# First halves of W1 and W3 in two buffers instead of three, in the expert stage of a hybrid decoder step

## The chip, the cores and the metric

One core of one Trainium2 chip. A time is the device time of one execution in microseconds (us); the kernel before has a median of 1078.21 us over three runs (1077.11 to 1081.03). All tensors are float32.

## The reference

One layer for 512 prompt tokens and 8 decode tokens (520 rows of 1024). Three branches (gated short convolution, stick-breaking attention, cross-attention on a memory) are merged through sigmoid gates and added to the input. Then comes a mixture of 32 experts, of which each token uses two:

```
x1 = x + sum(gates * branch) @ w_o
h  = rms_norm(x1, norm2)
g_idx = argmax(h @ w_group + b_group)              # 1 of 4 groups
top_v, top_i = top_k(router logits of that group, 2)   # 2 of its 8 experts
gate = softmax(top_v) * g_prob[g_idx]
y[t] = sum over the 2 experts e of  gate * ((silu(h[t] @ w1[e]) * (h[t] @ w3[e])) @ w2[e])
out = x1 + y
```

w1 and w3 are 1024x512 for each expert and w2 is 512x1024, so each of the three is 2 MiB, 6 MiB for one expert and 192 MiB for all.

## The kernel before

The first part (to about 590 us) makes the projections, the attention branches, the merge, x1, h and the routing. The rest is the expert stage, which the change touches. In it every expert n from 0 to 31 is computed for up to 64 token slots; what does not fit goes to extra blocks at the end, run only if there are any.

TensorE runs one round for each expert, in the order written out at L1452 to L1488. In a round it first waits for the gathered and transposed rows, then does `up_and_gate` (L1381): two parts of four K chunks, each chunk two matmuls of 128x512, one for W1 (L1389) and one for W3 (L1390), which run in two halves of the array beside each other. Before each part it waits for the weights of that part, and after each part it raises the semaphore `up_ps`. Then it gives back two pieces of the expert before (`give`, L1424), transposes the activations (L776), gives back a third piece, does `down` (the W2 matmuls, L1414 and L1415), which raises `y2_ps`, and gives back the fourth. VectorE, ScalarE and GpSimd evict, activate, add the pieces to x1 and build the selection matrices beside it. GpSimd gathers the rows of two experts at a time (`xg`, an indirect DMA from `h_dram`).

The weights have three buffers each (`WS = 3`, L61; L235 to L237): expert n uses buffer n % 3 of W1, W3 and W2, called w_a, w_b, w_c in the profile (the profile's name does not tell W1 from W3 and W2; the lines do). SyncE (SP) issues all weight DMAs on one queue, in program order. `load_up` (L540) issues W1 and W3 in two parts of 1 MiB each, in the order first half of W1, first half of W3, second half of W1, second half of W3; `load_expert` (L579) then issues W2 as one DMA of 2 MiB at L583. Before each it waits for the buffer to come free: for the first halves of expert n+3 until the first part of expert n is done (`up_ps` at 2n+1), for the second halves until the second part is done (2n+2), for W2 until `down` of expert n is done (`y2_ps` at n+1). Experts 0, 1 and 2 are loaded ahead of this loop, at L552 to L577, between the DMAs of the stages before: the first and second halves of W1 of expert 2 at L568, those of W3 of expert 2 and then W2 of expert 2 at L576 and L577, when the routing has passed `row_ps`. The DMAs at L548 are all those of W1 and W3.

Of the kernel before, what the change touches and what calls it, by code (L numbers as in the profile page):

```python
# [29 lines left out]
KD = D // P  # L30
# [9 lines left out]
NE = NG * EPG  # L40
# [20 lines left out]
WS = 3  # L61
# [25 lines left out]
def build(nc, io):  # L87
    ctx = ExitStack()
    with ctx:
# [7 lines left out]
        def place(name, region, offset, shape, dt=F32):  # L97
            return nc.alloc_sbuf_tensor_at(name, [P] + list(shape), dt, offset=at[region] + offset)
# [12 lines left out]
        def sem(name):  # L111
            return ctx.enter_context(nc.semaphore(name))
# [122 lines left out]
        w1_sb = [place("w1_a", "t", 0, [KD, DE]), place("w1_b", "ws", 16384, [KD, DE]), place("w1_c", "xn", 0, [KD, DE])]  # L235
        w3_sb = [place("w3_a", "t", 16384, [KD, DE]), place("w3_b", "qk", 0, [KD, DE]), place("w3_c", "ys", 0, [KD, DE])]
        w2_sb = [place("w2_a", "ws", 0, [CW, D]), place("w2_b", "qk", 16384, [CW, D]), place("w2_c", "xn", 16640, [CW, D])]  # L237
# [39 lines left out]
        first = route("first", [1])  # L277
# [55 lines left out]
        def bank(b, n=1):  # L333
            return acc_all[:, b * 512:(b + n) * 512]
# [10 lines left out]
        def tok(tt):  # L345
# [45 lines left out]
        lg_ps, lg_ok, lg_max, lg_exp, pick_ok, rank_ps, dest_ok, ids_ps, ids_ok, over_ok = (  # L391
            sem(n) for n in ("lg_ps", "lg_ok", "lg_max", "lg_exp", "pick_ok", "rank_ps",
                             "dest_ok", "ids_ps", "ids_ok", "over_ok"))
        w13_ld = [[sem(f"w13_ld{j}{part}") for part in "ab"] for j in range(WS)]
        w2_ld = [sem(f"w2_ld{j}") for j in range(WS)]
        xgt_ps, xgt_sb, up_ps, up_ok, upt_ps, sig_ok, half_ok, actt_ok, y2_ps = (sem(n) for n in (
            "xgt_ps", "xgt_sb", "up_ps", "up_ok", "upt_ps", "sig_ok", "half_ok", "actt_ok", "y2_ps"))
# [46 lines left out]
        def _(sp):  # L444
# [72 lines left out]
            w1_d = io["w1"].rearrange("e (p k) n -> e p k n", p=P)  # L517
            w3_d = io["w3"].rearrange("e (p k) n -> e p k n", p=P)
            w2_d = io["w2"].rearrange("e (p c) n -> e p c n", p=P)
# [14 lines left out]
            for j in range(RING):  # L534
                n = 2 * KD + j
# [1 line left out]
                sp.dma_start(w_raw[:, j, :, :], io["w_in"][IN_CHUNKS + RING + n]).then_inc(w_ld[j], 16)  # L537
                load_branch(n + RING)

            def load_up(e, j, *which, before=None):  # L540


                for part in range(2):
                    if before is not None:
                        sp.wait_ge(up_ps, 2 * before + part - 1)
                    ks = slice(part * KD // 2, (part + 1) * KD // 2)
                    for tiles, dram in (which,) if which else ((w1_sb, w1_d), (w3_sb, w3_d)):
                        sp.dma_start(tiles[j][:, ks, :], dram[e][:, ks, :]).then_inc(w13_ld[j][part], 16)  # L548


            sp.wait_ge(mid_st, MID_STORES)
# [13 lines left out]
                             x1[0:NB, NT - 1, half * DE:(half + 1) * DE]).then_inc(acc_ld, 16)  # L565
            sp.wait_ge(wo_ps, NT - 1)
            load_up(1, 1, w3_sb, w3_d)
            load_up(2, 2, w1_sb, w1_d)  # L568
            sp.wait_ge(wo_ps, 2 * NT)
            load_up(0, 0, w1_sb, w1_d)  # L570
            sp.wait_ge(h_ok, NT)
# [1 line left out]
            sp.dma_start(w2_sb[1][:, :, :], w2_d[1]).then_inc(w2_ld[1], 16)  # L573
            sp.wait_ge(h_st, 16 * NT)
            sp.wait_ge(row_ps, 1)
            load_up(2, 2, w3_sb, w3_d)  # L576
            sp.dma_start(w2_sb[2][:, :, :], w2_d[2]).then_inc(w2_ld[2], 16)  # L577

            def load_expert(e, j, before):  # L579
                load_up(e, j, before=before)  # L580

                sp.wait_ge(y2_ps, before)
                sp.dma_start(w2_sb[j][:, :, :], w2_d[e]).then_inc(w2_ld[j], 16)  # L583

            with sp.Fori(0, NE // WS - 1) as i:
                for j in range(WS):
                    load_expert(WS * i + WS + j, j, WS * i + j + 1)
            for e in range(NE // WS * WS, NE):
                load_expert(e, e % WS, e - WS + 1)

            sp.wait_ge(over_ok, 1)
            n_extra = sp.value_load(over_i[0:1, EXTRA:EXTRA + 1], min_val=0, max_val=EXTRA)
            with sp.If(n_extra > 0):
                with sp.Fori(0, EXTRA // 2) as i:
                    with sp.If(n_extra > 2 * i):
                        for j in range(2):
                            e = sp.value_load(over_i[0:1, bass.ds(2 * i + j, 1)], min_val=0, max_val=NE - 1)
# [176 lines left out]
        def _(pe):  # L774
# [3 lines left out]
            def warm_up(times, b=0):  # L778

                for _ in range(times):  # L780
                    pe.matmul(bank(b)[:, 0:P], ident[:, :], ident[:, :], start=True, stop=True)
# [346 lines left out]
            for h in range(HEADS):  # L1128
                pair, second = divmod(h, 2)
                n = KD + h  # L1130
# [44 lines left out]
            with pe.Fori(0, KD // RING) as i:  # L1175
                for j in range(RING):
                    n = 2 * KD + RING * i + j
# [200 lines left out]
                    pe.wait_ge(xgt_sb, 2 * p + half)  # L1378
                turn_pair(p % 2, half)

            def up_and_gate(w, slot, j, loads, n=None):  # L1381

                for part in range(2):
                    if n == 0:
                        pe.wait_ge(row_sb, part + 2)
                    pe.wait_ge(w13_ld[w][part], 32 * loads)
                    for k in range(part * KD // 2, (part + 1) * KD // 2):
                        lhs = xg_t[:, slot, k, CAP * j:CAP * (j + 1)]
                        pe.matmul(bank(5)[0:CAP, :], lhs, w1_sb[w][:, k, :], start=(k == 0), stop=(k == KD - 1))  # L1389
                        mm = pe.matmul(bank(5)[CAP:P, :], lhs, w3_sb[w][:, k, :], start=(k == 0), stop=(k == KD - 1))  # L1390
                    mm.then_inc(up_ps, 1)
                    if n == 0 and part == 0:
                        pe.wait_ge(dest_ok, GATED)
                        find(at_pos, lambda m, r, c: pick_of[0:m, r, c, :], NE, bank(2)).then_inc(ids_ps, 1)
                    if n == 1 and part == 0:
                        pe.wait_ge(dest_ok, OVER_SET)
                        find(over_pos, lambda m, r, c: over_in[0:m, r, c, :, :].rearrange("p a b -> p (a b)"), 2 * EXTRA,
                             bank(0)).then_inc(ids_ps, 1)
# [53 lines left out]
            for n in range(NE):  # L1452
                p, j = divmod(n, 2)
                if n >= 1:
                    pe.wait_ge(xgt_sb, 2 * p + 2)
                    pe.wait_ge(up_ok, n)
                up_and_gate(n % WS, p % 2, j, n // WS + 1, n)
                if n >= 1:
                    give(n - 1, (0, 1))
                else:  # L1460
                    warm_up(2)
                pe.wait_ge(up_ok, n + 1)
                turn_up()
                if n == 0:
                    warm_up(3)
                if n == 1:
                    turn_rows(1, 0)
                elif 2 <= n < NE - 2:
                    if n > BATCH and n % BATCH == 1:
                        pe.wait_ge(few_ok, 4 * (n // BATCH))  # L1470
                    turn_rows(p + 1, j)
                if n >= 1:
                    give(n - 1, (2,))
                if n == NE - 1:
                    give(n - 1, (3,))
                if n >= 1:
                    pe.wait_ge(rest_ok, n)
                down(n % WS, n // WS + 1, n)
                if n == 1:
                    turn_rows(1, 1)  # L1480
                if 1 <= n < NE - 1:
                    give(n - 1, (3,))
                if n >= BATCH and n % BATCH == 0:
                    give_few(n // BATCH - 1)
# [8 lines left out]
            with pe.If(n_extra > 0):  # L1493
                with pe.Fori(0, EXTRA // 2) as i:
                    with pe.If(n_extra > 2 * i):
                        for half in range(2):
                            if half == 0:
                                pe.wait_ge(xg_ld[0], 16 * (PAIRS // 2 + 1) + 16 * i)
                            pe.wait_ge(xgt_sb, NE + half + 2 * i)
                            pe.sem_inc(carried_pe, 1)  # L1500
                            turn_pair(0, half)
                        pe.wait_ge(xgt_sb, NE + 2 + 2 * i)
                        for j in range(2):
                            pe.wait_ge(up_ok, NE + j + 2 * i)
                            pe.sem_inc(carried_pe, 1)
                            loads = -(-NE // WS) + 1 + j + 2 * i
                            up_and_gate(0, 0, j, loads)
                            pe.wait_ge(up_ok, NE + j + 1 + 2 * i)
                            pe.sem_inc(carried_pe, 1)
                            turn_up()  # L1510
                            pe.wait_ge(actt_ok, 2 * (NE + j) + 2 + 4 * i)
                            pe.wait_ge(rest_ok, NE + j + 2 * i)
                            pe.sem_inc(carried_pe, 1)
                            down(0, loads)
                            pe.wait_ge(spread_ok, NE + j + 1 + 2 * i)
                            pe.wait_ge(rest_ok, NE + j + 1 + 2 * i)
                            for t in range(PIECES):
                                pe.wait_ge(back_ok, PIECES * (NE + j) + t - 1 + 2 * PIECES * i)
                                pe.sem_inc(carried_pe, 1)
                                give_back(t, j, (PIECES * j + t) % 2)  # L1520
# [1182 lines left out]
```

## Time and profile before

| | us |
|---|---|
| median of three runs | 1078.21 |
| profiled execution, device time | 1076.84 |
| its span, first to last instruction | 1075.0 |
| TensorE busy | 1041.4 (97%) |
| VectorE busy | 587.0 |
| ScalarE busy | 318.9 |
| DMA moved | 278.38 MB, mean 259 GB/s |

The profiled execution lies 1.37 us below the median of the three runs. The span is cut by the page into 40 slices of 26.9 us; the expert stage fills slices 23 to 40. Landing times are counted from the start of the DMA's issue.

### The profile page before, as it was taken

What the parts mean: (1) busy time and instruction counts of PE and PEld (TensorE: products, weight loads), DVE (VectorE), ACT (ScalarE), POOL (GpSimd) and SP (SyncE); (2) the same over time, 40 slices, a digit from 0 to 9 for tenths busy, and PEclk for the clock granted to TensorE, in tenths of its full rate; (3) what the DMA queues carried; (4) which work ended last, traced back from release to release, by engine and by line L of the source; (5) the groups of instructions that cost most, each with busy time, mean ns of one, the idle gap of its engine ahead of it and who ended that gap; (6) DMA issues with size and microseconds to landing.
All of it is one profiled execution on the core that took longest, in us unless ns stands there. A gap on an engine that the chain in (4) does not pass through costs nothing.

```text
span 1075.0 us, 16267 instructions
## 1 busy us (share of the span) xinstructions
PE 1041.4 (97%) x6646; PEld 697.9 (65%) x6646; DVE 587.0 (55%) x939; ACT 318.9 (30%) x470; POOL 148.6 (14%) x180
## 2 busy tenths in 40 slices
PE   8999999999999999999999999999999999999994
PEld 8999998988868777999775444444333344433331
DVE  5222255887756765433546655556555655555555
ACT  6322242164546544322343011111111111111110
POOL 0000000012303564000000311101111110111110
PEclk9999999999999999999999999999999999999998
DMA  5622131645442232651445999999999999999962
GB/s 201 262 90 98 64 99 57 217 129 190 157 183 87 92 106 80 221 205 66 162 179 225 424 423 425 426 426 427 426 425 425 428 429 423 426 426 427 426 296 80
DMA packets 51254, 278.38 MB, mean 259 GB/s; under 512 B 7538, under 2 KB 7810, under 8 KB 30708
## 3 DMA queue, kind: packets, MB, share of 16 engines
q1 hardware_dynamic: 42516, 254.79, 58.8%
q0 software_dynamic: 6048, 16.86, 4.4%
q10 hardware_dynamic: 2624, 5.80, 1.5%
q8 instruction: 48, 0.79, 0.3%
q14 instruction: 18, 0.15, 0.0%
HBM read 274.04 MB, written 7.48 MB: 262 GB/s over the span
## 4 chain that ended last, share of the span: by engine, by line
PE 88%; DVE 4%; DMA 3%; POOL 2%; issue 2%; ACT 2%; ACTq 0%; SPq 0%; DVEq 0%; POOLq 0%
PE acc_all L809 26%; PE acc_all L1389 20%; PE acc_all L1414 10%; PE acc_all L1424 7%; PE acc_all L776 6%; PE acc_all L955 5%; PE acc_all L1202 4%; DMA vals<-in_cache_mem_v 1%; PE acc_all L1005 1%; DMA xg<-h_dram,pair_row 1%; POOL beta L437 1%; PE acc_all L1073 1%; PE acc_all L1327 1%; PE acc_all L1415 1%; PE acc_all L885 1%
## 5 line engine op out<-in xcount | busy, mean ns | idle before, releaser
L809 PE MATMUL acc_all<-xn_hi,w_hi 128*128 128x260 f32 x832 | 171.5, 287 | 6.0 <-DVE gate_sb L2114 2.4
L809 PE MATMUL acc_all<-xn_hi,w_lo 128*128 128x260 f32 x832 | 168.0, 284 | 0.0
L809 PE MATMUL acc_all<-xn_lo,w_hi 128*128 128x260 f32 x832 | 167.8, 283 | 0.0
L2554 DVE TENSOR_TENSOR x<-x,acc_all 128x1024 f32<-128x1024 f32 x128 | 152.7, 1215 | 1.0 <-PE acc_all L1424 0.9
L809 PEld LDWEIGHTS acc_all<-xn_hi,w_hi 128*128 128x128 f32 x832 | 128.9, 189 | 13.9 <-issue 7.0
L809 PEld LDWEIGHTS acc_all<-xn_hi,w_lo 128*128 128x128 f32 x832 | 128.8, 189 | 0.0
L809 PEld LDWEIGHTS acc_all<-xn_lo,w_hi 128*128 128x128 f32 x832 | 128.7, 189 | 0.0
L733 POOL TENSOR_SCALAR spread<-tok_row,slots 128x512 fp32r<-128x512 f32 x32 | 50.1, 1566 | 370.3 <-PE acc_all L1424 370.2
L1944 DVE TENSOR_TENSOR w_lo<-w_raw,w_hi 128x1024 fp32r<-128x1024 f32 x52 | 63.4, 1222 | 67.8 <-ACT w_hi L1561 67.6
L1861 ACT ACTIVATE few<-acc_all,slots 8x512 f32<-8x512 f32 x64 | 43.4, 678 | 153.1 <-PE acc_all L1415 121.0
L1855 ACT ACTIVATE gate_h<-acc_all 128x256 f32<-128x256 f32 x32 | 12.3, 383 | 235.6 <-PE acc_all L776 235.6
L1389 PE MATMUL acc_all<-w_a,xg_t 128*64 128x512 f32 x176 | 78.1, 595 | 0.6 <-DVE xg_t L2443 0.6
L1389 PE MATMUL acc_all<-w_b,xg_t 128*64 128x512 f32 x176 | 78.1, 595 | 0.4 <-DVE xg_t L2526 0.4
L1390 PE MATMUL acc_all<-w_a,xg_t 128*64 128x512 f32 x176 | 78.1, 595 | 0.0
L1390 PE MATMUL acc_all<-w_b,xg_t 128*64 128x512 f32 x176 | 78.1, 595 | 0.0
L2537 DVE COPY up_sb<-acc_all 128x512 f32<-128x512 f32 x32 | 22.1, 692 | 100.3 <-PE acc_all L1390 100.1
L2549 DVE SCALAR_TENSOR_TENSOR y_rest<-acc_all,slots,y_top 128x512 fp32r<-128x512 f32 x32 | 24.0, 751 | 86.0 <-ACT y_top L1865 86.0
L1389 PE MATMUL acc_all<-w_c,xg_t 128*64 128x512 f32 x160 | 70.8, 595 | 0.1
L1390 PE MATMUL acc_all<-w_c,xg_t 128*64 128x512 f32 x160 | 70.8, 595 | 0.0
L1424 PE MATMUL acc_all<-y_top,spread 64*128 64x512 f32 x256 | 60.8, 470 | 4.0 <-DVE x L2554 2.2
L1424 PEld LDWEIGHTS acc_all<-y_top,spread 64*128 64x128 f32 x256 | 24.0, 183 | 60.6 <-issue 28.5
L1561 ACT ACTIVATE w_hi<-w_raw 128x1024 fp32r<-128x1024 f32 x52 | 54.5, 1050 | 7.5 <-DMA w_raw<-in_w_in 7.5
(387 smaller groups left out, 1863.5 us busy)
## 6 DMA issues: line engine op xcount, KB each, us to landing
w_a<-in_w SPq DMA_DIRECT2D x44, 1024.0 KB, 16.4
w_b<-in_w SPq DMA_DIRECT2D x44, 1024.0 KB, 17.0
w_c<-in_w SPq DMA_DIRECT2D x40, 1024.0 KB, 16.8
w_raw<-in_w_in SPq DMA_DIRECT2D x52, 512.0 KB, 3.7
w_a<-in_w SPq DMA_DIRECT2D x11, 2048.0 KB, 17.4
w_b<-in_w SPq DMA_DIRECT2D x11, 2048.0 KB, 18.9
w_c<-in_w SPq DMA_DIRECT2D x10, 2048.0 KB, 18.3
w_br<-in_w_branch SPq DMA_DIRECT2D x24, 256.0 KB, 4.5
```

The lines of the kernel that those rows point to most:

```text
L733: pool.tensor_scalar(spread[n % 2][:, :], tok_row[:, :], slot_tok[:, n:n + 1], None, ALU.is_equal).then_inc(spread_ok, 1)
L776: return pe.transpose(out, in_, ident[0:k, 0:k])
L809: mm = pe.matmul(out[:, a, :], w[:, slot, k, :], x[:, k, a * HALF_TOK:(a + 1) * HALF_TOK], start=first, stop=last)
L955: mm = pe.matmul(out[:, a, :], w, x[:, a * HALF_TOK:(a + 1) * HALF_TOK], start=begin, stop=end)
L1389: pe.matmul(bank(5)[0:CAP, :], lhs, w1_sb[w][:, k, :], start=(k == 0), stop=(k == KD - 1))
L1390: mm = pe.matmul(bank(5)[CAP:P, :], lhs, w3_sb[w][:, k, :], start=(k == 0), stop=(k == KD - 1))
L1414: pe.matmul(bank(7)[0:CAP, :], act_t[:, c, :], w2_sb[w][:, c, 0:DE], start=(c == 0), stop=(c == CW - 1))
L1424: mm = pe.matmul(bank(2 * pair + half), spread[hot][at, tok(t)], y[at, :], start=first, stop=not first)
L1561: act.activation(w_hi[:, slot, :, :], w_raw[:, slot, :, :], ACT.Copy).then_inc(split_hi, 1)
L1861: act.activation(few[n // QUADS % 2][half][strip:strip + NB, :], bank(7)[at, :], ACT.Copy, scale=slot_gate[at, n:n + 1]).then_inc(few_in, 1)
L1944: dve.tensor_tensor(w_lo[:, slot, :, :], w_raw[:, slot, :, :], w_hi[:, slot, :, :].bitcast(F32), ALU.subtract).then_inc(split_lo, 1)
L2554: dve.tensor_tensor(x1[:, t, :], x1[:, t, :], bank(2 * pair, 2), ALU.add).then_inc(back_ok, 1)
```

## The change

Only the first halves (K chunks 0 to 3) of W1 and W3 change their buffer: expert n uses buffer n % 2 for them, and buffer n % 3 for the second halves and for W2, as before. The space of the third buffer's first half stays unused. The first halves of expert 2 are no longer loaded ahead of the loop. A round n of requests is now: first halves of expert n+2 after the first part of expert n, second halves of expert n+3 after its second part, W2 of expert n+3 after its `down`. One more request, the first halves of expert 31, follows the last round. The semaphores follow the buffers, and SP's loop is written out instead of being a loop at run time. TensorE's work is the same.

```diff
-        w13_ld = [[sem(f"w13_ld{j}{part}") for part in "ab"] for j in range(WS)]
+        WA = 2
+        w13_ld = [[sem(f"w13_lda{j}") for j in range(WA)], [sem(f"w13_ldb{j}") for j in range(WS)]]
...
+            def load_half(e, part, slot, *which):
+
+                ks = slice(part * KD // 2, (part + 1) * KD // 2)
+                for tiles, dram in (which,) if which else ((w1_sb, w1_d), (w3_sb, w3_d)):
+                    sp.dma_start(tiles[slot][:, ks, :], dram[e][:, ks, :]).then_inc(w13_ld[part][slot], 16)
+
+            def load_up(e, j, *which):
+
+                load_half(e, 0, j, *which)
+                load_half(e, 1, j, *which)
...
             load_up(1, 1, w3_sb, w3_d)
-            load_up(2, 2, w1_sb, w1_d)
+            load_half(2, 1, 2, w1_sb, w1_d)
...
-            load_up(2, 2, w3_sb, w3_d)
+            load_half(2, 1, 2, w3_sb, w3_d)
             sp.dma_start(w2_sb[2][:, :, :], w2_d[2]).then_inc(w2_ld[2], 16)
...
-            with sp.Fori(0, NE // WS - 1) as i:
-                for j in range(WS):
-                    load_expert(WS * i + WS + j, j, WS * i + j + 1)
-            for e in range(NE // WS * WS, NE):
-                load_expert(e, e % WS, e - WS + 1)
+            def load_round(n, first, second):
+
+                sp.wait_ge(up_ps, 2 * n + 1)
+                load_half(n + WA, 0, first)
+                sp.wait_ge(up_ps, 2 * n + 2)
+                load_half(n + WS, 1, second)
+                sp.wait_ge(y2_ps, n + 1)
+                sp.dma_start(w2_sb[second][:, :, :], w2_d[n + WS]).then_inc(w2_ld[second], 16)
+
+            for n in range(NE - WS):
+                load_round(n, n % WA, n % WS)
+            sp.wait_ge(up_ps, 2 * (NE - WA - 1) + 1)
+            load_half(NE - 1, 0, (NE - 1) % WA)
...
-                    pe.wait_ge(w13_ld[w][part], 32 * loads)
+                    w = ws[part]
+                    pe.wait_ge(w13_ld[part][w], 32 * loads[part])
...
-                up_and_gate(n % WS, p % 2, j, n // WS + 1, n)
+                up_and_gate((n % WA, n % WS), p % 2, j, (n // WA + 1, n // WS + 1), n)
```

## Rows read from the trace of the kernel before

**Rows 1.** The page, part 2: the span in 40 slices.
```profile
PE   8999999999999999999999999999999999999994
DMA  5622131645442232651445999999999999999962
```
**Rows 2.** Waits of all engines from 590 us: engine, line, what it waited for, us.
```profile
POOL spread L733 <- PE acc_all L1424: 370.2, 30, 12.9
...
PE acc_all L1424 <- DVE x L2554: 2.2, 3, 1.9
...
PEld acc_all L776 <- DMA xg<-h_dram,pair_row: 1.0, 1, 1.0
```
**Rows 3.** The chain that ended last, first matmul of experts 28 and 31: start, us, what.
```profile
1000.91 0.57 PE acc_all L1389
...
1043.96 0.57 PE acc_all L1389
```
**Rows 4.** Busy time by stretches: us, engines, PE clock, DMA share, GB/s.
```profile
544.00:562.00 18.00, 17.87 (x111) 14.79 (x110) 8.27 (x38) 6.72 (x14) 0.00 (x0) 1.00 0.68 267
...
601.00:613.00 12.00, 10.90 (x87) 4.79 (x85) 5.95 (x20) 0.38 (x1) 2.99 (x5) 1.00 1.02 427
...
627.00:642.00 15.00, 14.90 (x78) 5.99 (x76) 8.43 (x17) 2.43 (x4) 2.56 (x2) 1.00 1.02 424
642.00:1030.00 388.00, 385.36 (x1958) 154.87 (x1956) 214.22 (x308) 64.47 (x107) 53.87 (x40) 1.00 1.01 426
```
**Rows 5.** SyncE's requests from 545 us: start, us, line, tile, count.
```profile
545.06 1.15 SPq L548 DMA_DIRECT2D w_c<-in_w  x2
...
589.13 0.80 SPq L548 DMA_DIRECT2D w_c<-in_w  x2
589.98 0.44 SPq L577 DMA_DIRECT2D w_c<-in_w  x1
594.75 5.76 SPq L548 DMA_DIRECT2D w_a<-in_w  x4
```
**Rows 6.** Line L548, the request at 573.84 alone, and its landing.
```profile
L548 SPq DMA_DIRECT2D w_a<-in_w x1: 328/328/328, 573.8 to 573.8; - x1
DMA to landing us min/median/max: 4.9/4.9/4.9
```
**Rows 7.** Line L548, the request of W1 at 628.6, and its landing.
```profile
L548 SPq DMA_DIRECT2D w_c<-in_w x1: 332/332/332, 628.6 to 628.6; - x1
DMA to landing us min/median/max: 7.7/7.7/7.7
```
**Rows 8.** Line L548, first halves of experts 29, 30, 31 (W3 is the later).
```profile
L548 SPq DMA_DIRECT2D w_c<-in_w x2: 333/354/376, 976.0 to 976.4; - x2
...
DMA to landing us min/median/max: 24.0/25.5/27.0
...
L548 SPq DMA_DIRECT2D w_a<-in_w x2: 338/382/426, 990.2 to 990.6; - x2
DMA to landing us min/median/max: 24.6/26.9/29.1
...
L548 SPq DMA_DIRECT2D w_b<-in_w x1: 432/432/432, 1004.9 to 1004.9; - x1
DMA to landing us min/median/max: 29.5/29.5/29.5
```
**Rows 9.** Line L583, W2 of expert 28, then of 30 and 31, with landings.
```profile
L583 SPq DMA_DIRECT2D w_b<-in_w x1: 333/333/333, 971.6 to 971.6; - x1
DMA to landing us min/median/max: 26.8/26.8/26.8
...
L583 SPq DMA_DIRECT2D w_a<-in_w x1: 328/328/328, 1000.3 to 1000.3; - x1
L583 SPq DMA_DIRECT2D w_b<-in_w x1: 511/511/511, 1014.6 to 1014.6; - x1
...
DMA to landing us min/median/max: 29.2/29.3/29.5
```

More of the change, by code:

```diff
@@ L538, in _ @@
                 load_branch(n + RING)
[L540 to L548, printed above, removed]
+            def load_half(e, part, slot, *which):
[5 more added lines that the diff above has]
+                load_half(e, 1, j, *which)
             sp.wait_ge(mid_st, MID_STORES)
@@ L575, in _ @@
             sp.wait_ge(row_ps, 1)
-            load_up(2, 2, w3_sb, w3_d)
+            load_half(2, 1, 2, w3_sb, w3_d)
             sp.dma_start(w2_sb[2][:, :, :], w2_d[2]).then_inc(w2_ld[2], 16)
[L579 to L583, printed above, removed]
-            with sp.Fori(0, NE // WS - 1) as i:
-                for j in range(WS):
-                    load_expert(WS * i + WS + j, j, WS * i + j + 1)
-            for e in range(NE // WS * WS, NE):
-                load_expert(e, e % WS, e - WS + 1)
+            def load_round(n, first, second):
[9 more added lines that the diff above has]
+            load_half(NE - 1, 0, (NE - 1) % WA)
             sp.wait_ge(over_ok, 1)
@@ L1379, in turn_rows, with up_and_gate @@
                 turn_pair(p % 2, half)
-            def up_and_gate(w, slot, j, loads, n=None):
+            def up_and_gate(ws, slot, j, loads, n=None):
                 for part in range(2):
@@ L1506, in _ @@
                             loads = -(-NE // WS) + 1 + j + 2 * i
-                            up_and_gate(0, 0, j, loads)
+                            up_and_gate((0, 0), 0, j, (NE // WA + 1 + j + 2 * i, loads))
                             pe.wait_ge(up_ok, NE + j + 1 + 2 * i)
```

## The prediction

> **What bounds the kernel now.** I read the slices of the page first [rows 1]. From the 23rd slice on, the expert stage, TensorE is at 90% or more and the 16 DMA engines are too, so the two limits have to be told apart. The waits do that [rows 2]: from 590 us on TensorE waits for no weight DMA at all. Its longest waits are 2.2 us in all for VectorE's additions to x1 and 1.0 us for the first gather of rows, while GpSimd waits 370 us for TensorE. The chain of waits agrees: the first matmul of expert 28 starts at 1000.91 and that of expert 31 at 1043.96 [rows 3], so a round of TensorE takes (1043.96 - 1000.91) / 3 = 14.35 us, and experts 29 and 30 start at 1015.26 and 1029.61.
>
> The landings show how close the transfers are behind. W2 of expert 30 lands at 1000.3 + 29.2 = 1029.5 and W2 of expert 31 at 1014.6 + 29.5 = 1044.1 [rows 9], so the 6 MiB of one expert take 14.65 us with no gather among them: 2.44 us for 1 MiB. W2 of expert 28 lands at 971.6 + 26.8 = 998.4, so over three experts and the gather or two that fall among them it is (1044.1 - 998.4) / 3 = 15.2 us an expert. The transfers are 0.3 to 0.9 us a round slower than TensorE. They are saturated from 601 us on (share 1.01, 426 GB/s from 642 to 1030) [rows 4], and what keeps TensorE from waiting is a lead built before the stage, which is eaten up: a request made at 628.6 lands 7.7 us later [rows 7], one made at 1014.6 lands 29.5 us later [rows 9], since requests are made at TensorE's pace and served at the queue's. At the end of the kernel before some lead is left: the first halves of expert 31 land at 1004.9 + 29.5 = 1034.4 [rows 8] and are used at 1043.96, 9.6 us later. This change spends from that lead.
>
> **The change part by part.** TensorE's matmuls, the other engines and the bytes moved are the same, so everything lies in when weights land. I write a(n) for the first halves of W1 and W3 of expert n, b(n) for the second, 2 MiB each, 4.9 us.
>
> *The loads ahead of the loop.* a(2) is 2 MiB in two pieces. The piece of W1 was requested in the pair at 545.06, in a stretch with DMA share 0.68 [rows 4, 5]: it was free, and is now transferred inside the saturated stretch, +2.44 us of queue. The piece of W3 was in the pair at 589.13, ahead of W2 of expert 2 at 589.98 [rows 5]. It moves to the first round at 594.75. Without it 3 MiB (7.3 us and the start-up) are still queued at 589.13, so the queue reaches past 594.75 and the engines don't idle for it. That piece only moves within the saturated stretch: 0 in total, and everything up to the last W2 lands 2.44 us earlier than it did. a(2) itself, asked for at 594.75, is used by expert 2 some 30 us later and is no danger.
>
> *The order in a round.* The events that SP waits for are the same, and each round still requests 2 + 2 + 2 MiB at the same three points; only a(n+2) stands where a(n+3) stood. So a(n) of the changed kernel takes the place in the queue that a(n+1) has now, with b(n) and W2 of the same expert ahead of it, and becomes the last piece of its expert to land. Places are read off the landings of now, less 2.44 us:
> a(28): 976.4 + 27.0 - 2.44 = 1000.96, needed at 1000.91: 0.05 us late.
> a(29): 990.6 + 29.1 - 2.44 = 1017.26, needed at 1015.26: 2.0 late.
> a(30): 1034.4 - 2.44 = 1031.96, needed at 1029.61: 2.35 late.
> a(31), the new last request, stands behind W2 of expert 31: 1044.1 - 2.44 + 2 x 2.44 = 1046.6, needed at 1043.96: 2.6 late [rows 3, 8, 9].
> These don't add up: TensorE once late by 2.0 at expert 29 is late by 0.35 more at 30 and 0.3 more at 31. The sum is the last one, +2.6 us. The second halves and W2 land ahead of a(n), so no other wait is new. What stands behind a late a(31) on TensorE is the whole of expert 31 and the pieces of 30, 31 us to the end of the span, and nothing shortens it.
>
> *The wait that SP gains.* The last request waits for `up_ps` of expert 29. Behind it stand only the stores of the output. With a(29) used by 1017.3 + 3.5, it is made at about 1021, when b(31) and W2 of 31 (until 1041.7) are still queued: 0. Writing SP's loop out can move a request by some tenths of a us either way; each lands 7.7 us or more after it is made [rows 7 to 9], with others queued ahead, so it is worth 0 unless the cover of the next part is used up.
>
> *A queue with less in it.* At every moment 1 MiB less is queued. The place to look is the shallowest one, the request at 628.6. A 1 MiB request that meets an empty queue lands after 4.9 us [rows 6]; this one lands after 7.7 [rows 7], so 2.8 us of work stood before it. In the changed kernel it is 2.8 - 2.44 = 0.36 us. So the queue just does not run dry by this sum. Each us that it does is lost for good and comes back at expert 31, where transfers now set the end. Lower bound 0, as a queue with less in it moves no byte sooner; upper bound from the same rows: an idle start-up of 2.4 us (4.9 less 2.44) in one round. I take 0, the row itself.
>
> *The size of the piece.* 2.44 us is a mean. Landings of W1 and W3 pieces are uneven, since the slowest of the 16 engines ends each. Costing the W1 piece at nothing gives 0.2 us late, and at the whole pair's 4.9 gives 5.1. I take the mean.
>
> *The first gather* (1.0 us of wait, rows 2) now has 1 MiB less before it. It may bring TensorE forward by up to 1.0 us, but as transfers set the end that is not kept.
>
> Sum: span 1075.0 + 2.6 = 1077.6. The profiled execution had 1.84 us around its span: 1079.5. It lies 1.37 below the median of the runs, so on that median 1078.2 + 2.6 = 1080.8.
>
> The Trainium skill, "Trainium Kernel Development and Optimization", section Best Practices, asks to double-buffer so that DMA overlaps compute. By it two buffers are enough and the change is worth 0. The rows speak against using it here: a round's transfers take longer than its matmuls, and then depth is a reserve. It is the first rival below.
>
> The same skill's page "DMA: Bandwidth & Descriptors", section Bandwidth, gives 435 GB/s as the ceiling of the ports. The trace has 426 to 428. At that ceiling the 455 us of transfers would end some 8 us sooner and no wait would arise.
>
> **The rivals.**
> *No wait reaches the end.* Two first-half buffers cover the round. For it: the lateness of 2.6 us is 0.6% of the 455 us of saturated transfers between 589 and 1044, so a queue that much faster in an unprofiled execution hides it all. Against: 426 GB/s holds over 388 us. Time: 1078.2, or 1077.2 with the gather's gain.
> *The queue runs dry early.* In the first rounds, around 610 to 645 us, engines finish before the next request. It decides when more than the 0.36 us of cover is missing, and costs an idle start-up of 2.4 us in one round, up to twice that if two rounds are hit: 2.6 + 2.4 to 4.8 = 5.0 to 7.4 late, 1083.2 to 1085.6. For it: the thin cover, and the share of 1.01 is a mean over 16 engines. Against: transfers are slower than rounds, so the queue deepens from there (7.7 us to landing at 628.6, 29.5 us at the end) [rows 7, 9], and one round at most should be hit.
> *Faster.* Less queued ahead of the gathers, each used sooner, and nothing late: at most the 1.0 us above; the 2.2 us for VectorE [rows 2] are not touched. No path to 5 us.
> *The change does not do what it says.* If a(n+2) in fact met an idle queue, a(n) would land right after its request, 14 us before use, and the time would be the first rival's.
>
> **How the numbers follow.** A run of this kernel can be told from no change at about 0.5%, 5.4 us. Forecast (late by 0.5 to 5.4 us, 1080.8): 0.63. No wait at the end: 0.20. Dry queue beyond 1083.6: 0.13. Faster than 1072.8: 0.04. So within 0.5% is 0.83, slower 0.13, faster 0.04. The range takes in the first rival with the gather's gain (1077.2) and one dry round (1083.2), to 1083.9.
>
> **What would show it.** TensorE waiting for weight DMAs at L1389, about 2 us before expert 29, and 0.3 to 0.4 each before 30 and 31; a(31) landing last of all weights at about 1046.6, W2 of 31 at about 1041.7; DMA share 1.0 without a gap from 601. Waits from expert 20 on, or a share under 0.95 between 610 and 645, would mean the dry queue. No wait on weights would mean the first rival. A wait at experts 2 to 4 would show my reading of the start wrong.

## The result and the profile after

Over 11 runs of each the changed kernel has a median of 1080.49 us (1079.52 to 1084.45), the kernel before 1079.03 (1076.86 to 1081.03). The ratio is 1.0024, with a 95% interval of 1.0013 to 1.0035: 2.6 us slower (1.4 to 3.8). In a second set of runs it was 1.0025 (1.0016 to 1.0035). The forecast was +2.6 us, 1080.8.

The profiled execution of the changed kernel took 1080.03 us with a span of 1078.3, against 1076.84 and 1075.0. TensorE's busy time is 1041.5 us, as before, so the 3.3 us are waits. The slices of its page (TensorE, the DMA engines, and what they moved) answer to [rows 1]:

```profile
PE   8999999999999999999999999999999999999995
...
DMA  5622231645442232651436999999999999999972
GB/s 200 259 93 97 65 98 57 219 127 199 156 173 89 97 110 71 230 209 47 162 139 246 412 408 428 425 427 427 428 427 424 427 428 428 426 425 428 429 308 80
```

Slices 23 and 24, the first of the expert stage, stand at 412 and 408 GB/s, while those behind them have 424 to 429; in the kernel before slices 23 to 38 all have 423 or more. (The last two slices are lower in both kernels, since the transfers end there.) The view of what TensorE waited for from 1000 us on answers to [rows 2]. Two of its rows (the second and the fourth) are new: 2.9 us in four waits, all for weights and all at the first matmul of W1. Before 1000 us there is no such wait.

```profile
PE acc_all L1429 <- DVE x L2559: 2.2, 3, 1.9
PE acc_all L1394 <- DMA w_a<-in_w: 1.8, 2, 1.3
PE acc_all L1429 <- DVE y_rest L2554: 1.7, 1, 1.7
PE acc_all L1394 <- DMA w_b<-in_w: 1.1, 2, 0.7
```

The requests of first halves of experts 28 to 31 and their landings, from the view of line L545, answer to [rows 8]. Each pair is followed by the wait that it ended, then by its landings (the largest number is the later piece, W3):

```profile
L545 SPq DMA_DIRECT2D w_a<-in_w x2: 328/380/433, 976.2 to 976.6; - x2
  PE acc_all L1394: 1.3, 1
DMA to landing us min/median/max: 23.2/24.5/25.9
...
L545 SPq DMA_DIRECT2D w_b<-in_w x2: 328/677/1026, 990.6 to 990.9; - x2
  PE acc_all L1394: 0.4, 1
DMA to landing us min/median/max: 23.6/24.9/26.3
...
L545 SPq DMA_DIRECT2D w_a<-in_w x2: 328/380/433, 1006.2 to 1006.6; - x2
  PE acc_all L1394: 0.6, 1
DMA to landing us min/median/max: 22.5/24.1/25.6
...
L545 SPq DMA_DIRECT2D w_b<-in_w x2: 328/380/433, 1021.0 to 1021.4; - x2
  PE acc_all L1394: 0.7, 1
DMA to landing us min/median/max: 22.5/24.2/26.0
```

So a(28) lands at 976.6 + 25.9 = 1002.5, a(29) at 1017.2, a(30) at 1032.2, a(31) at 1047.4. The last landing before, W2 of 31, is at 1016.3 + 26.1 = 1042.4. The chain of waits, followed back from the last instruction, crosses to the transfers twice near the end (it then holds the time from a request to its landing); before it stayed on TensorE [rows 3]:

```profile
990.92 26.29 DMA w_b<-in_w
1017.21 0.14 issue
1017.35 0.61 PE acc_all L1394
...
1021.40 25.96 DMA w_b<-in_w
1047.37 0.14 issue
1047.50 0.61 PE acc_all L1394
```

Expert 31 starts at 1047.5 instead of 1043.9. The stage itself starts 0.3 us later in this execution (its first matmul at 591.2, before 590.9), which is not put down to the change: the second profiled execution of the same kernel starts it at 592.5, and in the fourteen profiles of this document it lies between 590.9 and 593.5. To compare executions I use from here on the time from the first matmul of expert 0 to that of expert 31: 453.0 us before, 456.3 after. These are differences of rows rounded to 0.1 us and can be off by that much.

### The profile page after: what moved, and what is told of

It is laid out like the page before. It is cut to its first block, busy times and chain, and to the rows that moved or that the text cites. A ratio compares the mean times of both kernels' runs of the same rounds, so it can differ in the third digit from the quotient of the medians.

```text
span 1078.3 us, 16032 instructions
## 1 busy us (share of the span) xinstructions
PE 1041.5 (97%) x6646; PEld 699.4 (65%) x6646; DVE 586.9 (54%) x939; ACT 318.8 (30%) x470; POOL 148.7 (14%) x180
## 4 chain that ended last, share of the span: by engine, by line
PE 83%; DMA 6%; DVE 4%; POOL 2%; issue 2%; ACT 2%; SPq 0%; ACTq 0%; DVEq 0%; POOLq 0%
PE acc_all L813 26%; PE acc_all L1394 19%; PE acc_all L1419 9%; PE acc_all L1429 6%; PE acc_all L780 5%; PE acc_all L959 5%; DMA w_b<-in_w 5%; PE acc_all L1206 4%; POOL beta L438 1%; DMA vals<-in_cache_mem_v 1%; PE acc_all L1009 1%; PE acc_all L1077 1%; PE acc_all L1331 1%; POOL keep L438 1%; PE acc_all L1420 1%
## 5 line engine op out<-in xcount | busy, mean ns | idle before, releaser
L1394 PE MATMUL acc_all<-w_a,xg_t 128*64 128x512 f32 x216 | 97.1, 596 | 2.5 <-DMA w_a<-in_w 1.8
L1394 PE MATMUL acc_all<-w_b,xg_t 128*64 128x512 f32 x216 | 97.1, 596 | 1.5 <-DMA w_b<-in_w 1.1
L1395 PE MATMUL acc_all<-w_b,xg_t 128*64 128x512 f32 x216 | 97.1, 596 | 0.0
L1395 PE MATMUL acc_all<-w_a,xg_t 128*64 128x512 f32 x216 | 97.1, 596 | 0.0
L1394 PEld LDWEIGHTS acc_all<-w_b,xg_t 128*64 128x64 f32 x216 | 28.2, 137 | 60.6 <-issue 59.4
L1394 PEld LDWEIGHTS acc_all<-w_a,xg_t 128*64 128x64 f32 x216 | 28.2, 137 | 59.7 <-issue 58.5
## 6 DMA issues: line engine op xcount, KB each, us to landing
w_a<-in_w SPq DMA_DIRECT2D x11, 2048.0 KB, 16.7
```

## The experiments

Fourteen rows stand in this table, for twelve kernels; the two above are among them, and two kernels were run twice. The second column is from the timed runs, the third from the one profiled execution. Ratios are to the kernel before, timed in the same set of runs on the same chip.

| kernel | ratio (95% interval) | expert 0 to 31, us |
|---|---|---|
| before | 1 | 453.0 |
| after | 1.0024 (1.0013, 1.0035) | 456.3 |
| after, again | 1.0025 (1.0016, 1.0035) | 456.4 |
| e1, only the order | 1.0040 (1.0027, 1.0053) | 457.2 |
| e2, only the late start | 0.9990 (0.9982, 0.9999) | 452.8 |
| e3, only the loop written out | 1.0003 (0.9994, 1.0012) | 453.6 |
| e4, second halves in two | 1.0033 (1.0020, 1.0046) | 457.2 |
| e5, W2 in two | 1.0019 (1.0008, 1.0029) | 458.5 |
| e6, all in two | 1.0037 (1.0024, 1.0050) | 456.7 |
| e7, 2 MiB more in round 12 | 1.0087 (1.0074, 1.0100) | 461.2 |
| e7, again | 1.0073 (1.0060, 1.0086) | 461.7 |
| e8, 2 MiB less | 1.0000 (0.9991, 1.0009) | 452.9 |
| e9, 2 MiB more in round 0 | 1.0058 (1.0046, 1.0070) | 459.7 |
| e10, a(31) ahead | 1.0018 (1.0005, 1.0031) | 456.5 |

**Are transfers what sets the end?** Three kernels change only the bytes of the changed kernel. e8 loads only half of W2 of experts 15 and 16, and so leaves out part of what these two give to the output:

```diff
+                cs = slice(0, CW // 2) if n in (12, 13) else slice(0, CW)
-                sp.dma_start(w2_sb[second][:, :, :], w2_d[n + WS]).then_inc(w2_ld[second], 16)
+                sp.dma_start(w2_sb[second][:, cs, :], w2_d[n + WS][:, cs, :]).then_inc(w2_ld[second], 16)
```

> The changed kernel with 2 MiB less to load: of W2 of experts 15 and 16 only the first half is loaded, so what these two experts give to the output is left out in part; TensorE's work is the same. Theory: all landings after it are 4.9 us sooner, so no wait for weights is left (they were 2.9 us in all) and the time is that of the kernel before within 0.3 us. Rival (the price lies elsewhere): 2.6 us slower than before stays.

The ratio is 1.0000, and TensorE waits for no weight. e7 loads 2 MiB more into the unused space:

```diff
+                if n == 12:
+                    for tiles, dram in ((w1_sb, w1_d), (w3_sb, w3_d)):
+                        sp.dma_start(tiles[2][:, 0:KD // 2, :], dram[0][:, 0:KD // 2, :]).then_inc(more_ld, 16)
                 load_half(n + WA, 0, first)
```

> The changed kernel with 2 MiB more to load: in round 12 first halves of W1 and W3 of expert 0 are loaded again into the unused third buffer, and nobody reads them. Theory (transfers set the end): all landings after it are 4.9 us later, so 4.9 us slower than the changed kernel, 7.5 to 8 us slower than before (1.007), with the waits for weights starting near expert 23. Rival (TensorE's own rounds or the start of the stage make the 2.6 us): no more than 0.5 us slower than the changed kernel, 1.0024 to 1.003.

The ratio is 1.0087, and expert 31 starts 461.2 us into the stage, 4.9 later than in the changed kernel: the transfer time of 2 MiB, as expected. The waits for weights begin earlier than I expected, at expert 20 and not near 23, and are eleven, 7.6 us together. The time grew by more than 4.9, 0.0087 - 0.0024 = 0.0063 or 6.8 us. The rest stands in the last expert. These are the stretches of its pieces and of its W2 matmuls in e7 (us, busy times, granted clock, DMA share, GB/s), then the same two of the changed kernel:

```profile
1061.60:1066.90 5.30, 3.27 (x22) 1.83 (x20) 4.73 (x8) 0.38 (x1) 0.00 (x0) 1.00 0.00 0
1066.90:1072.60 5.70, 5.42 (x18) 1.47 (x16) 1.61 (x2) 0.23 (x1) 0.00 (x0) 0.70 0.00 0
```

```profile
1054.50:1059.80 5.30, 3.25 (x22) 1.83 (x20) 4.77 (x8) 0.38 (x1) 0.00 (x0) 1.00 0.00 0
1059.80:1065.50 5.70, 4.03 (x22) 1.43 (x22) 2.33 (x3) 1.15 (x2) 0.00 (x0) 1.00 0.00 0
```

TensorE is granted 1.2 GHz for part of the W2 matmuls in e7 (0.70 of 2.4 GHz as a mean) and 2.4 in the other. From the start of expert 31 to the end of the span it is 1087.2 - 1054.6 = 32.6 us in e7 and 30.8 in the changed kernel. This comes in some executions only: the profiled ones of e1, e4 and e6 had it (0.70), those of before, after, e2, e3, e5, e8, e9 and e10 did not. To have e7 and its base on one chip I ran both again.

> The changed kernel once more, beside the three others of this set on the same chip, as their base. 2 to 3 us slower than before.

> The changed kernel with 2 MiB more in round 12, once more. Its first halves of expert 31 landed 4.9 us later than in the changed kernel once the start of the stage is put equal, yet the time grew by 6 to 7 us, and in its profile TensorE was granted 0.70 of its clock in 5.7 us of the last expert's W2 matmuls, which cost 1.8 us. Theory: 4.9 us by the transfers, and the rest by that clock, which comes in some executions and not in others: 4.9 to 7 us slower than the changed kernel. Rival: the extra bytes cost more than their transfer time, and the first halves of 31 land 6 us later.

The ratios are 1.0025 and 1.0073: 5.2 us apart, near the 4.9 of the transfers. This time the profiled execution of the changed kernel itself has the low clock in its W2 matmuls (0.78, and 32.4 us from expert 31 to the end instead of 30.8), so the clock is no property of e7:

```profile
1061.20:1066.90 5.70, 5.12 (x20) 1.33 (x16) 1.65 (x2) 0.52 (x1) 0.00 (x0) 0.78 0.00 0
```

**What of the change costs?** e2 keeps three buffers and the old order and only takes the first halves of expert 2 from the loads ahead:

```diff
                 sp.wait_ge(up_ps, 2 * n + 1)
+                if n == 0:
+                    load_half(2, 0, 2)
+                load_half(n + WS, 0, first)
```

> Three buffers and the order of the kernel before; only the first halves of expert 2 are no longer loaded ahead but asked for in the first round, just before those of expert 3. Theory: 1 MiB moves into the saturated stretch, all later landings are 2.44 us later, and the first halves of expert 31 land at about 1036.9, 7 us before use: no difference from before (within 0.3 us). Rival (the lost load is the price): 2.6 us slower.

There is no cost (0.9990; if anything it is 1 us faster, which I don't explain). The late start alone is inside the lead. e3 writes SyncE's loop out:

```diff
-            with sp.Fori(0, NE // WS - 1) as i:
-                for j in range(WS):
-                    load_expert(WS * i + WS + j, j, WS * i + j + 1)
-            for e in range(NE // WS * WS, NE):
+            for e in range(WS, NE):
                 load_expert(e, e % WS, e - WS + 1)
```

> The kernel before with SyncE's loop over the rounds written out, and nothing else. Theory: no difference (within 0.3 us). Rival (the written-out loop, with its instructions fetched beside the weights, costs or gives time): a difference of 1 us or more.

The ratio is 1.0003, no difference. e1 takes the new order alone, with everything loaded ahead as before:

```diff
+        WA = 3
...
+            load_up(2, 2, w1_sb, w1_d)
...
+                if n >= 1:
+                    sp.wait_ge(up_ps, 2 * n + 1)
+                    load_half(n + 2, 0, (n + 2) % WA)
```

> Three buffers for everything and expert 2 loaded whole ahead of the loop, as in the kernel before; only the order of a round is the changed kernel's (first halves of n+2, second halves of n+3, W2 of n+3, and the first halves of expert 31 as the last request). Theory (the end is set by when the first halves of expert 31 land, last in the queue): they land 2.44 us sooner than in the changed kernel (1047.4), about 1044.5, used at 1043.96: 0 to 1 us slower than before, a ratio of 1.000 to 1.001, with waits of under 1 us for weights at experts 28 to 31. Rival (only the load that was lost ahead of the loop costs, the order nothing): no wait for weights at all. Rival (the order is the whole price): 2.6 to 3 us slower, 1.0024 or more.

My theory's number failed: I expected at most 1 us and measured 1.0040, 4.3 us, with a(31) landing 457.1 us into the stage, against 456.2 in the changed kernel. 2 MiB more lay loaded ahead of the loop, and nothing came sooner. The reason is in the early rounds. From round 1 on, e1 and the changed kernel have asked for exactly the same bytes at the same events, and in round 0 e1 asks for 2 MiB less. So its queue runs empty, and from an empty queue on, landings follow the times of the requests, whatever was loaded before. The first stretch of e1 shows it plainly (DMA share 0.87 and 325 GB/s, the last two figures; before 1.02 and 427 [rows 4]):

```profile
601.00:613.00 12.00, 10.81 (x68) 4.70 (x69) 6.46 (x21) 0.38 (x1) 2.91 (x5) 1.00 0.87 325
```

That its last landing is even 0.9 us later than that of the changed kernel isn't explained by this in full: 0.4 us of it stand already at W2 of expert 5 (57.9 us into the stage against 57.5). The stretch from 615 to 645 us in 40 slices of 0.75 us shows the same more finely, DMA share in tenths and GB/s, for the kernel before, the changed kernel and e1:

```profile
DMA  9999999999999999999889999999999999999999
GB/s 415 382 404 404 437 415 437 437 426 404 437 415 415 426 426 415 459 470 513 371 360 426 415 404 426 404 459 415 437 426 415 426 437 404 437 371 426 470 415 393
```

```profile
DMA  9899999999999997997997989999999999998989
GB/s 344 360 388 399 404 399 415 448 415 459 404 415 382 437 371 251 393 393 306 393 426 317 404 371 470 393 470 404 404 470 393 448 393 470 426 492 371 481 371 415
```

```profile
DMA  6999999999999897999999499999999999999899
GB/s 262 393 399 453 394 437 415 448 393 437 415 426 448 360 470 295 404 415 393 459 426 219 142 371 382 415 404 426 437 426 437 415 437 415 448 339 350 350 415 415
```

Before it is even, but for two 8s. In the changed kernel the share falls to 7 in three slices between 626 and 632, around the request at 628.6; in e1 to 6, 7 and 4, down to 142 GB/s. In coarse stretches the share of the changed kernel does not show this, only its GB/s do, as the next experiment has it. The request of W1 at 628.6 in the changed kernel answers to [rows 7]; it lands 0.6 us sooner after its issue than before, not 2.44:

```profile
L545 SPq DMA_DIRECT2D w_a<-in_w x1: 328/328/328, 628.6 to 628.6; - x1
DMA to landing us min/median/max: 7.1/7.1/7.1
```

**Is that gap real, and what is it worth?** e9 puts the 2 MiB of e7 into round 0 (`if n == 0` instead of 12), where they can fill it.

> The changed kernel with the same 2 MiB more, but asked for in round 0, ahead of the first halves of expert 2, and nobody reads them. Theory (the queue of the changed kernel runs partly dry between 601 and 642, where it moved 0.7 MB less than the kernel before): the extra bytes fill that gap, so of their 4.9 us some 1 to 2 are free: the first halves of 31 land 3 to 4 us later than in the changed kernel, and the time is 1 to 2 us below the kernel with the same bytes in round 12. Rival (the queue is never dry, the 0.8 us by which the last landing missed the forecast are only the engines' unevenness): the same 4.9 us, no difference between the two.

The ratio is 1.0058 against 1.0073: the same bytes cost 1.6 us less. The two intervals overlap, but both kernels ran in one set on one chip, and the slowest of e9's six executions (1086.07) is below the fastest of e7's five (1086.30). Expert 31 starts 2.0 us sooner than in e7 again (459.7, 461.7). Busy time in three early stretches of the changed kernel, then of e9, then the second of them in the kernel before:

```profile
601.00:613.00 12.00, 11.02 (x85) 4.97 (x84) 6.26 (x20) 0.38 (x1) 2.99 (x5) 1.00 1.02 416
613.00:627.00 14.00, 13.77 (x82) 6.04 (x80) 9.12 (x16) 4.47 (x7) 1.57 (x1) 1.00 1.01 394
627.00:642.00 15.00, 14.90 (x78) 6.00 (x76) 8.44 (x17) 2.42 (x4) 2.40 (x2) 1.00 1.00 412
```

```profile
601.00:613.00 12.00, 11.02 (x78) 4.98 (x78) 6.47 (x21) 0.38 (x1) 2.99 (x5) 1.00 1.01 426
613.00:627.00 14.00, 13.77 (x90) 6.23 (x88) 8.89 (x16) 4.48 (x7) 1.57 (x1) 1.00 1.01 426
627.00:642.00 15.00, 14.90 (x78) 5.92 (x76) 8.44 (x17) 2.43 (x4) 2.19 (x2) 1.00 1.01 428
```

```profile
613.00:627.00 14.00, 13.78 (x80) 5.95 (x78) 9.26 (x16) 4.47 (x7) 1.57 (x1) 1.00 1.00 421
```

416, 394 and 412 GB/s are 16.7 MB in 41 us; e9's 426 to 428 are 17.5. The 0.8 MB between them are 1.9 us of transfer, which is what e9 got for nothing. The queue of the changed kernel does run partly empty.

**Is it the last request only?** e10 asks for a(31) right behind a(30), into the unused buffer:

```diff
                 load_half(n + WA, 0, first)
+                if n == NE - WS - 1:
+                    load_half(NE - 1, 0, 2)
```

> The changed kernel, but the first halves of expert 31 go into the unused third buffer and are asked for in round 28, right behind those of expert 30 and ahead of the second halves and W2 of 31. Theory (every first half from expert 28 on is late by its place in the queue, and 31 adds only the last 0.7 us): the waits before 28, 29 and 30 stay (2.3 us together in the profile of the changed kernel), that before 31 goes: 0.5 to 0.8 us faster than the changed kernel. Rival (the last request is the whole price): no more than 0.3 us slower than before.

The rival falls: with the last request out of the way 1.0018 (1.0005 to 1.0031) stays. The wait before 31 is gone from the profile, and those before it sum to 3.3 us. The gain by the ratios is 0.7 us, as expected, but the intervals overlap, and the profiled execution shows none (456.5): its a(30) landed 0.9 us later in the stage than in the changed kernel. What the last request alone is worth is therefore not settled.

**Does it matter which buffer is given up?** e4 gives up the second halves, e5 gives up W2:

```diff
+                load_half(n + WS, 0, second)
                 sp.wait_ge(up_ps, 2 * n + 2)
+                load_half(n + WA, 1, first)
```

> The mirror of the change: the second halves of W1 and W3 in two buffers, the first halves in three, so as many bytes are given up, as much is no longer loaded ahead, and the last request is the second halves of expert 31. Theory: they land at the same 1046.6 to 1047.4, but TensorE needs them 3.4 us later than the first halves, at 1047.4: 0 to 0.4 us slower than before. Rival (2 MiB less of prefetch costs what it costs, whichever half): 2.6 us slower as in the changed kernel.

```diff
+                sp.dma_start(w2_sb[n % W2N][:, :, :], w2_d[n + W2N]).then_inc(w2_ld[n % W2N], 16)
```

> W2 in two buffers instead of three, W1 and W3 in three as before: it gives up the same 2 MiB as the change. The last request is W2 of expert 31. Theory: the early rounds have a shallower queue and may lose 1 to 5 us of transfer, so W2 of expert 31 lands at 1044 to 1049, but it is used only at 1056, and the first halves of expert 31 land before 1041: no wait for weights, and the time of the kernel before within 0.3 us. Rival (a shallower queue costs by itself): 2 us slower or more.

Both expectations failed: 1.0033 and 1.0019 where I said 0 to 0.4 us and none. In both I placed only the last piece. In e4 the last piece is in time (it lands at 1047.1 and is used at 1051.7), but b(30) is not. It stands behind a(31) now: 1034.4 - 2.44 + 4.9 = 1036.9 on the scale of the kernel before, needed at 1029.6 + 3.4 = 1033.0, so 3.9 us late; 0.0033 is 3.6 us. In the profile it landed 446.2 us into the stage, by that sum 1036.9 - 590.9 = 446.0. The chain of e4 ends its last crossing at b(30):

```profile
1011.99 25.38 DMA w_a<-in_w
```

In e5 it is W2 of 30, which the chain shows landing at 1045.8, 452.8 us into the stage. The kernel before uses it at 1039.65, 448.7 into its stage, 4.1 sooner:

```profile
1018.75 27.02 DMA w_a<-in_w
```

```profile
1039.65 0.61 PE acc_all L1414
```

The place alone does not make it late. All other weights but W2 of 31 come before it, so it takes the place of b(31), which landed at 1008.8 + 30.4 = 1039.2 in the kernel before, in time by 0.4 us. The rest is the queue: from 601 to 642 e5 moved 15.8 MB, the kernel before 17.4 MB, 3.6 us of transfer less. So in e5 the rival of my expectation came, a shallower queue costs by itself, and 0.0019 is its 2 us. The third column overstates it: the profiled execution (1084.14) lies 2.1 us above the median of its kernel, and around its 2.0 us of waiting for W2 of 30 TensorE was granted 0.70 of its clock in that execution, so that the first W2 matmuls took 1.06 to 1.09 us instead of 0.6:

```profile
1043.50:1049.20 5.70, 3.69 (x14) 1.27 (x12) 3.21 (x6) 0.00 (x0) 0.00 (x0) 0.70 0.52 220
```

One of e5's twelve timed executions took 5801.8 us. It is left out of the ratio; the trace is of another execution, so its cause is open.

In both kernels the last piece was in time and the last but one was not.

e6 has two buffers for everything (`WS = 2`, nothing of expert 2 ahead of the loop):

> All weights in two buffers: round n asks for first halves, second halves and W2 of expert n+2, and nothing of expert 2 is loaded ahead of the loop. Theory: the queue is dry between 589 and 595 and thin in the rounds after, but then as saturated as before, and W2 of 31, the last to land (about 1055), is used at 1056; the first halves of 31 land at 1045 to 1047: 1 to 3 us slower than before. Rival (each 2 MiB of buffer given up costs the 2.6 us of the change): 7.8 us slower, 1.007. Rival (two buffers are enough): no difference.

The ratio 1.0037 is 4.0 us (2.6 to 5.4): a bit over my 1 to 3, far under the rival's 7.8, and not zero. 6 MiB of buffer cost only 1.4 us more than 2 MiB, and the two intervals overlap. Once the queue has run empty, giving up more ahead of the loop hardly moves the landings: a(31) lands 456.6 us into the stage, 0.4 later than in the changed kernel. What more e6 loses stands behind the start of expert 31, where the third column does not reach: b(31) lands at 461.5, and TensorE waits 1.1 us for it.

## Why the prediction was right, and where not

The mechanism is the one forecast: the new waits are for weights only, only at the last experts, and do not add up to more than the lateness of a(31). e7 and e8 show that transfers set the end; e2 and e3 exclude the late start alone and the loop. That the sum fitted so closely is partly luck, as the third point says.

- *The sum.* +2.6 us forecast, 2.6 (1.4 to 3.8) measured. a(31) was to land at 1046.6, 455.7 us into the stage; it landed at 456.2, and at 456.2 again in the second profile of the kernel.
- *The single experts.* Forecast 0.05, 2.0, 0.35 and 0.3 us before experts 28 to 31; measured 1.3, 0.4, 0.6 and 0.7. The waits start an expert sooner, since a(28), with the starts of the stage put equal, landed 1.1 us later than its place, a(29) 0.4 sooner and a(30) within 0.1 us of theirs. The second profile of the same kernel has 0.2 us before expert 27 and 0.9, 1.5, 0 and 0.6 before 28 to 31: the single waits change from one execution to the next, their sum of some 3 us does not.
- *The queue with less in it* is the step that failed. I left 0.36 us of cover at 628.6 and took 0. The cover was missing: from 601 to 642 the kernel moved 0.69 MB less than the kernel before (416, 394, 412 against 427, 421, 424 GB/s), 1.6 us of transfer. The shallowest place was also not where I looked: of the 0.69 MB, 0.51 were missing before 627, and the request at 628.6 found more work before it than by my sum. It was to land after 7.7 - 2.44 = 5.3 us and landed after 7.1.

  That a(31) still missed its place by only 0.5 has a reason that I had not seen. The places were read off the last landings of the kernel before, less 2.44 us each. At the same places in the queue, counted from the start of the stage, the changed kernel landed W2 of 28 1.6 us sooner (405.9 against 407.4) and a(28) 1.4 sooner (411.2, 412.6), so about 1 us of the 2.44 was lost by then; but a(29) landed 2.8 sooner (426.0, 428.8), a(30) 2.5 (441.0, 443.5) and W2 of 31 1.9 (451.3, 453.2). From that place on the kernel before had itself fallen behind its own pace (6.4 us from the landing of W2 of 29 to the next pair's, where it had been 4.9 and 5.2 in the two rounds before), and this error of the places hid most of the other. Why it fell behind is not shown. The changed kernel also moved a little more in the long stretch, 161.28 MB against 161.04 from 642 to 1020, worth 0.6 us; why is not shown either. What is shown is the loss early in the stage, and by e9 that requests made there get 1.6 to 2 us back.
- *The free load* was reasoned with the wrong rule. I priced the W1 piece at 2.44 us because it moved into the saturated stretch. e1 shows that after a queue that runs empty nothing loaded ahead counts. Here both rules give nearly the same: a queue empty at 628.6 would give 4.9 - 2.8 = 2.1 us.
- *My sign for a dry queue* (a share under 0.95 between 610 and 645) was a bad one: in the changed kernel the share read 1.00 to 1.02 in stretches of 12 to 15 us while 3 to 6% fewer bytes moved than before. GB/s and 0.75 us slices showed it.
- *The rivals.* The first, two buffers suffice, is excluded: the interval leaves 1.4 us at the least. Of the second, the dry queue, the mechanism came (a partly empty queue early in the stage) but not the size: nothing beyond 5.4 us.

The Trainium skill ("Trainium Kernel Development and Optimization", Best Practices) asks to double-buffer so that DMA overlaps compute. It does not say that a third buffer is worth nothing, as I read it in the prediction, and here that reading fails: e6 has two buffers throughout and is 4.0 us slower than three, though for 6 MiB that may be a fair price.

## What to carry to other kernels

Where DMA is saturated but compute still sets the time, the lead of the loads is a stock that is eaten up: write down for each piece when it lands and when it is used, near the end, and take the worst of all pieces rather than the last one requested. Find where the queue is shallowest: where it ran empty, as in e1, what was loaded earlier was worth nothing, and only the times of the later requests counted. Giving up a buffer costs by the place of its pieces in the order of need (e4) and by what the queue leaves undone while it is shallow (e5), not by its bytes (e6).

## What the runs showed of the hardware

- Near saturation the DMA share of a stretch did not fall with the bytes moved (1.01 at 394 GB/s and 1.01 at 426, 613 to 627 us in the changed kernel and in e9); it did where the gap was larger (0.87 at 325 in e1).
- Issuing one weight DMA took SyncE 1.3 us at the most as long as less than 12 MiB of weights were requested and not yet landed, in all profiles of the stage. With 12 MiB or more some requests took longer: 2.7 us twice in the kernel before, up to 4.0 us in e2.
- The granted clock fell to 0.70 in the 5.7 us of the last expert's W2 matmuls in the profiled executions of e1, e4, e6 and e7, after a stretch in which TensorE was busy 3.3 to 4.0 of 5.3 us. In before, after and e8 it was 1.00 after the same 3.3 of 5.3, and in the second profile of the changed kernel 0.78 after the same. It cost 1.6 to 1.8 us from expert 31 to the end (32.4 and 32.6 against 30.8). What decides it stays open.
